# Expert rounds of a two-layer MoE backbone, unrolled and overlapped across rounds (Trainium2, one core)

## What is computed

```python
def expert_choice_ffn(h, router_w, w1, w3, w2):
    bsz, n, d = h.shape
    cap = n * EC_CAPACITY // N_EXPERTS              # 32 tokens for each of 16 experts
    aff = jax.nn.softmax((h @ router_w).astype(F32), axis=-1)
    gates, idx = lax.top_k(jnp.swapaxes(aff, 1, 2), cap)
    ...
    xe = jnp.take_along_axis(h, idx[..., None], axis=1).reshape(bsz, N_EXPERTS, cap, d)
    hid = jax.nn.silu(jnp.einsum('becd,edf->becf', xe, w1)) * jnp.einsum('becd,edf->becf', xe, w3)
    ye = jnp.einsum('becf,efd->becd', hid, w2) * gates[..., None].astype(h.dtype)
    return jnp.zeros_like(h).at[jnp.arange(bsz)[:, None], idx].add(ye.reshape(bsz, N_EXPERTS * cap, d))
```

## Time and profile before

| | us |
|---|---|
| median of 3 runs (2564.57 to 2569.61) | 2565.92 |
| the profiled execution, its own time | 2568.53 |
| its span on the core | 2566.8 |
| TensorE busy (share of the span) | 2026.7 (79%) |
| VectorE busy | 779.4 (30%) |
| ScalarE busy | 514.3 (20%) |
| DMA, mean over the span | 205 GB/s |
| chain that ended last: transfers of expert weights | 23% |
| chain that ended last: expert products (L883) | 11% |

### The profile page before, as it was taken

How to read it: one execution, slowest core, us unless ns; L and a number is a source line. 1 busy time by engine, 2 the same in 40 slices (tenths; PEclk the granted TensorE clock), 3 DMA queues, 4 the chain that set the end, 5 groups by cost and what they waited for, 6 DMA issues and landing times.

```text
span 2566.8 us, 31156 instructions
## 1 busy us (share of the span) xinstructions
PE 2026.7 (79%) x12656; PEld 1071.9 (42%) x12656; DVE 779.4 (30%) x1454; ACT 514.3 (20%) x1049; POOL 191.0 (7%) x230
## 2 busy tenths in 40 slices
PE   5899769987799588888888899949997955656655
PEld 1344554434444432323232566627786831212211
DVE  1011453337730310000010577756765120000001
ACT  1223331112210201010000333244442010000000
POOL 0000000012200000000000400004442000000000
PEclk8899889989999799999999999979998977878887
DMA  9701302160041169898989331110001239999996
GB/s 362 274 9 66 131 0 99 66 240 23 1 164 66 67 262 430 341 432 346 431 340 426 139 131 74 66 66 2 2 2 58 93 162 433 432 431 431 429 433 255
DMA packets 57497, 527.07 MB, mean 205 GB/s; under 512 B 2848, under 2 KB 4128, under 8 KB 43040
## 3 DMA queue, kind: packets, MB, share of 16 engines
q1 hardware_dynamic: 55760, 522.55, 49.1%
q10 hardware_dynamic: 1616, 2.76, 0.3%
HBM read 524.26 MB, written 1.05 MB: 205 GB/s over the span
## 4 chain that ended last, share of the span: by engine, by line
PE 54%; DMA 24%; DVE 9%; issue 4%; ACT 3%; SPq 3%; DVEq 1%; PEldq 0%; POOL 0%; POOLq 0%; PEld 0%; ACTq 0%
DMA ring<-in_moe_w 23%; PE bank L432 21%; PE bank L883 11%; PE bank L812 7%; SPq L283 2%; PE bank L868 2%; DVE ring L1581 2%; PE bank L536 2%; PE bank L619 1%; PE bank L642 1%; DVE x L1943 1%; DMA ring<-in_ab_w 1%; PE bank L405 1%; PE bank L929 1%; PE bank L823 1%
## 5 line engine op out<-in xcount | busy, mean ns | idle before, releaser
L432 PE MATMUL bank<-hT,ring 128*128 128x512 f32 (+1 forms) x1504 | 550.9, 524 | 11.4 <-ACT hT L1006 7.2
L883 PE MATMUL bank<-ring,xgs 128*32 128x512 f32 x3072 | 390.8, 666 | 140.4 <-DMA ring<-in_moe_w 132.0
L432 PEld LDWEIGHTS bank<-hT,ring 128*128 128x128 f32 x1504 | 283.8, 191 | 257.3 <-issue 240.1
L883 PE MATMUL bank<-ring,hT 128*32 128x512 f32 x1536 | 209.0, 701 | 95.3 <-DMA ring<-in_moe_w 95.2
L883 PEld LDWEIGHTS bank<-ring,xgs 128*32 128x32 f32 x3072 | 110.6, 121 | 409.1 <-issue 300.4
L1770 DVE TENSOR_TENSOR hT<-sils,bank 128x512 f32<-128x512 f32 x24 | 15.8, 685 | 601.7 <-PEq L911 601.7
L883 PEld LDWEIGHTS bank<-ring,hT 128*32 128x32 f32 x1536 | 57.3, 126 | 241.5 <-issue 191.7
L1776 DVE SCALAR_TENSOR_TENSOR x<-bank,modT,x 128x256 f32<-128x256 f32 x96 | 42.5, 480 | 320.5 <-PE bank L929 320.5
L1435 DVE SCALAR_TENSOR_TENSOR x<-gluR,cols,x 128x256 f32<-128x256 f32 x240 | 116.0, 483 | 15.9 <-issue 0.4
L1244 ACT ACTIVATE sils<-bank 128x512 f32<-128x512 f32 x24 | 13.5, 596 | 331.4 <-PEq L904 331.3
L385 PE MATMUL bank<-ring,act_c 128*32 128x512 f32 x384 | 56.1, 743 | 26.3 <-DMA ring<-in_mod_w 24.5
(11 more groups left out here) (440 smaller groups left out, 2473.6 us busy)
## 6 DMA issues: line engine op xcount, KB each, us to landing
ring<-in_moe_w SPq DMA_DIRECT2D x96, 4096.0 KB, 21.8
ring<-in_mod_w SPq DMA_DIRECT2D x48, 1024.0 KB, 14.2
ring<-in_cd_w SPq DMA_DIRECT2D x6, 4096.0 KB, 17.9
ring<-in_ab_w SPq DMA_DIRECT2D x5, 4096.0 KB, 21.8
ring<-in_ab_wo SPq DMA_DIRECT2D x2, 4096.0 KB, 18.4
ring<-in_cd_wo SPq DMA_DIRECT2D x2, 4096.0 KB, 12.4
x<-in_xT SPq DMA_DIRECT2D x1, 2048.0 KB, 10.2
ring<-in_ab_w SPq DMA_DIRECT2D x1, 2048.0 KB, 15.7
```

Source lines behind the costliest of these rows:

```text
L432: last = mm(ps[p["no"] % 4][:, p["c0"]:T], w[:, k, :], hT[:, k, p["c0"]:T], start=(k == 0), stop=(k == KD - 1))
L883: last = mm(ps[banks + s][32 * j:32 * j + 32, :], lhs[s][:, 4 * kh + k, 32 * j:32 * j + 32], w[:, j, k, :], start=(kh == 0 and k == 0), st ...
```

## The change

The loops over q on TensorE, ScalarE and VectorE become Python loops, so all four rounds stand in the instruction streams one after the other. The operations are the same ones; their order on each engine changes, and `xg` gets a second buffer:
- the scatter steps of round q - 1 stand after the products of groups 0, 1, 2 and 3 of round q, two steps after each;
- the (up to) four half gathers of round q + 1 stand after the products of groups 6, 7, 8 and 9 of round q, in banks 4 and 7 alone;
- only the first round's gather stands ahead of its products, and only the last round's scatter behind them;
- the drains that counted `moe_h1`, `moe_h3` and `moe_y` go, and ScalarE and VectorE wait for `w_used` of the group in their place.

```diff
-            xgs = sb("xgs", [P, 2, KD, P], F32, st)
+            xgs = sb("xgs", [P, 2, 2, KD, P], F32, st)
+        def used(layer, q, gi):
+            return rg.first[f"moe{layer}"] + 12 * q + gi + 1
+        def gathered(layer, streams, q, b):
+            return 16 * layer + 2 * len(streams) * q + b
 # TensorE
-                with pe.Fori(0, Q) as q:
-                    pe.wait_ge(sg("moe_added"), 8 * q + 8 * q0)
...
+                def gather(q, b):
+                    if q >= Q or b >= 2 * len(streams):
+                        return
+                    s, half = streams[b // 2], b % 2
+                    no = gathered(layer, streams, q, b)
+                    if b >= 2:
+                        pe.wait_ge(sg("moe_xg"), no - 1)
+                    elif q > 0:
+                        pe.wait_ge(sg("moe_added"), 8 * (Q * layer + q - 1))
+                    for k in range(4):
+                        ch = (4 * half + k) * P
+                        for tt in range(2):
+                            last = mm(ps[(4, 7)[half]][:, k * P:(k + 1) * P], htok[:, 2 * s + tt, ch:ch + P], pick[:, s, tt, P * q:P * q + P],
+                                      start=(tt == 0), stop=(tt == 1), skip_group_check=True)
+                    last.then_inc(sg("gathered"), 1)
...
+                def scatter(q, steps):
+                    if q < 0:
+                        return
+                    done = Q * layer + q
+                    for dt in steps:
+                        if dt % 4 == 0:
+                            pe.wait_ge(sg("moe_ycopied"), 2 * done + dt // 4 + 1)
+                        if 8 * done + dt >= 2:
+                            pe.wait_ge(sg("moe_added"), 8 * done + dt - 1)
...
+                for b in range(4):
+                    gather(0, b)
+                for q in range(Q):
+                    n = 2 * (Q * layer + q)
+                    pe.wait_ge(sg("moe_xg"), gathered(layer, streams, q + 1, 0))
+                    if n:
+                        pe.wait_ge(sg("moe_tcopied"), n)
+                    product(q, 0, 0, xg[q % 2], 0)
+                    scatter(q - 1, (0, 1))
+                    product(q, 1, 1, xg[q % 2], 0)
+                    scatter(q - 1, (2, 3))
+                    if n:
+                        pe.wait_ge(sg("moe_ycopied"), n)
+                    product(q, 2, 0, xg[q % 2], 2)
+                    scatter(q - 1, (4, 5))
+                    product(q, 3, 1, xg[q % 2], 2)
+                    scatter(q - 1, (6, 7))
+                    pe.wait_ge(sg("moe_silu"), n + 1)
+                    product(q, 4, 0, xg[q % 2], 0)
+                    product(q, 5, 1, xg[q % 2], 0)
+                    turn(q, 0, 5)
+                    product(q, 6, 0, xg[q % 2], 2)
+                    gather(q + 1, 0)
+                    product(q, 7, 1, xg[q % 2], 2)
+                    gather(q + 1, 1)
+                    pe.wait_ge(sg("moe_tcopied"), n + 1)
+                    product(q, 8, 0, hidT, 5)
+                    gather(q + 1, 2)
+                    turn(q, 1, 0)
+                    product(q, 9, 0, hidT, 2)
+                    gather(q + 1, 3)
+                    pe.wait_ge(sg("moe_tcopied"), n + 2)
+                    product(q, 10, 1, hidT, 5)
+                    product(q, 11, 1, hidT, 2)
+                scatter(Q - 1, range(KD))
 # ScalarE: gate waits for w_used of group 4 * hf + 1, result for that of group 10 + hd
+                for b in range(4):
+                    gather(0, b)
+                for q in range(Q):
+                    gate(q, 0)
+                    gate(q, 1)
+                    turned(q, 0)
+                    gather(q + 1, 0)
+                    gather(q + 1, 1)
+                    gather(q + 1, 2)
+                    turned(q, 1)
+                    gather(q + 1, 3)
+                    result(q, 0)
+                    result(q, 1)
 # VectorE: hidden waits for w_used of group 4 * hf + 3
+                for q in range(Q):
+                    add(q - 1, range(6))
+                    hidden(q, 0)
+                    add(q - 1, (6, 7))
+                    hidden(q, 1)
+                add(Q - 1, range(KD))
```

More of the change, by code:

```diff
@@ L854, in experts @@
                 first = rg.first[f"moe{layer}"]
-                q0 = Q * layer
-                with pe.Fori(0, Q) as q:
-                    pe.wait_ge(sg("moe_added"), 8 * q + 8 * q0)
[L859 to L889, removed]
-                        for s in streams:
[L891 to L923, removed]
@@ new lines, in product @@
+                def product(q, gi, kh, lhs, banks):
+                    s = (first + gi) % RING
+                    pe.wait_ge(landed[s], q * 64 + rg.landed[first + gi])
+                    w = ring[:, s, :, :].rearrange("p j (k n) -> p j k n", k=4)
+                    for k in range(4):
+                        for s in streams:
+                            for j in range(4):
+                                last = mm(ps[banks + s][32 * j:32 * j + 32, :], lhs[s][:, 4 * kh + k, 32 * j:32 * j + 32],
+                                          w[:, j, k, :], start=(kh == 0 and k == 0), stop=(kh == 1 and k == 3),
+                                          tile_position=(0, 32 * j))
+                    last.then_inc(w_used, 1)
@@ new lines, in turn @@
+                def turn(q, hf, bank):
+                    pe.wait_ge(sg("moe_hid"), 2 * (Q * layer + q) + hf + 1)
+                    for s in streams:
+                        for b in range(4):
+                            last = nc.tensor.transpose(ps[bank + s][:, b * P:(b + 1) * P],
+                                                       hid[s][:, 512 * hf + b * P:512 * hf + b * P + P], ident[:, :])
+                    last.then_inc(sg("moe_turned"), 1)
+                def scatter(q, steps):
[3 more added lines that the diff above has]
+                    for dt in steps:
@@ L1230, in experts @@
             def experts(layer, streams):
[L1231 to L1256, removed]
@@ new lines, in gather, with gate @@
+                def gather(q, b):
+                    if q >= Q or b >= 2 * len(streams):
+                        return
+                    s, half = streams[b // 2], b % 2
+                    act.wait_ge(sg("gathered"), gathered(layer, streams, q, b) + 1)
+                    A_(xg[q % 2][s][:, 4 * half:4 * half + 4, :], ps[(4, 7)[half]].rearrange("p (k c) -> p k c", k=4),
+                       ACT.Copy).then_inc(sg("moe_xg"), 1)
+                def gate(q, hf):
+                    n = 2 * (Q * layer + q) + hf
+                    act.wait_ge(w_used, used(layer, q, 4 * hf + 1))
+                    if n:
+                        act.wait_ge(sg("moe_hid"), n)
+                    for s in streams:
+                        last = A_(sil[s], ps[s], ACT.Silu)
+                    last.then_inc(sg("moe_silu"), 1)
```

46 lines of the change are left out of this document (28 added, 18 removed).

## The result

The change takes 2531.14 us (median of 4 runs, 2528.47 to 2532.02) against 2565.31 us (median of 4, 2564.57 to 2569.61): a ratio of 0.9862 with a 95% interval of 0.9845 to 0.9879. That is 34.2 us faster, where 40.9 were forecast, and 6.1 us over the forecast time of 2525.0. The profiled execution took 2530.77 us with a span of 2529.0; the span before was 2566.8, so these two differ by 37.8, and 3.1 of the 40.9 us are missing there. That 37.8 is more than 34.2 comes mainly from the profiled execution of before, which lay 3.2 us over its median. The change measured once more, in a later set of runs, gave 2531.13 us against 2567.52 (0.9863, 0.9839 to 0.9887). In what follows, a ratio stands behind each time, with its 95% interval; it is to the kernel before, measured beside it.

What follows compares the result with a forecast made beforehand. Layer 0 was taken as bound by DMA inside rounds and TensorE's serial tail at three boundaries, layer 1 by its weights. 2568.5 - 40.9 = 2527.6 us for the profiled execution, 2525.0 against the median; range 2517 to 2540.

Steps and rivals of the forecast that it cites:

- The bound and its hole: Layer 0: DMA-bound inside rounds, a load hole of some 10 us at three boundaries costing 13.7 each; layer 1 has none.
- the ring: Layer 0 boundaries: three weight loads run on after a round's last group lands; then loads stop until a slot comes free.
- TensorE's sum: Layer 0: products, gathers, scatter and turns take 104.1 us a round, 109.3 with changes of form, below the DMA's 116.6.
- The 5.2 us for 18 changes of form: Layer 0, per round: switches between 32-column and full matmuls, 18 against 6 before, 0.29 us each at the worse end.
- The new waits: Waits of moved scatter, gather and copies on adds, copies and banks: no releaser later than its place in the product stream; 0.
- The stall at the loop's top: TensorE wait of 4.61 us without a releaser at a layer 0 boundary; goes with the loop, no separate gain.
- the 24.5 us: Serial boundary between layer 0 rounds: scatter of 8.29 us, rest of its adds, a stall of 4.61 us, and the gather.
- The sum: Layer 0: with loads never stopped, group 47 lands 349.7 us after group 11 started, at 1363.7 against 1404.64; gain 40.9 us.
- Layer 1, which I had at 0: Layer 1: transfers saturated from first round to last, so the overlap has no hole to fill; gain 0.
- A: Layer 0 partial gain: TensorE late from tile changes or a missed wait a round; gain 20 to 25 us, 2543; chance 0.09.
- B: No gain: loads stop elsewhere or the code does not overlap as written; rounds stay at 130 us, 2566; chance 0.03.
- C: Slower: unrolled streams are fetched anew, each fetch stalling TensorE 4.61 us in layer 0; +53 us, 2619; chance 0.05.

## Why the prediction was right, and where it was off

**The bound and its hole: right.** Layer 0 lost its time in a hole of the loads at three boundaries, layer 1 lost none. After the change the DMA share is 1.00 through rounds 1 to 3, and three other ways to shorten the boundary (17.4, 8.0 and about 8.3 us) gave what the ring says each should.

**TensorE's sum: right in size, its terms less so.** 104.1 us a round were forecast and 104.0 measured. That they agree to 0.1 us is luck: the gathers took 8.2 us in place of 9.1 (24.6 for three), since they no longer ran at the boundary's lower clock, and two products a round took 8.6 to 8.8 in place of 7.07. The 5.2 us for 18 changes of form were too many. I had taken the worse end, which came from a scatter behind a drain; the starts give 2.9 at most, and these are inside the 104.0. The room was 12.6 us. The Trainium skill says that changing the tiling mode drains TensorE (TensorEngine Tiling (Array Packing), Key Properties). The traces neither show nor exclude a drain: if there is one, it is part of the 0.16 us.

**The new waits: right.** None of them has idle time in the profile but the first gather's last copy, 0.7 us, as before.

**The stall at the loop's top: misjudged in what it was worth.** As "part of the 24.5 us" it could not change the sum, but the loop cost more than 4.61: with the lower clock and the slower gather behind the stall it took 7.1 us of the first boundary. Had the change been only to unroll, my reading would have said 14 us and the chip 25.

**The sum: the step that failed** is "with the loads never stopped, group 47 lands 36 x 9.714 = 349.7 us later". It landed 354.3 us later. 9.714 us was read from layer 1 before, where one page of instructions was fetched in those 36 loads; layer 0 fetches 22 in the same stretch. At 0.2 us each, as measured in layer 1, they would cost 4.4 us (an estimate; no version fetched fewer in layer 0). They were there before the change too, 27 in the same loads, and cost little, because each hole let the slower engines catch up: the distance between a load's first and last engine fell to 0.8 to 1.0 us behind each hole and never passed 2.1 us in layer 0 before, and it is at most 2.2 in the unrolled kernel with the serial order, which keeps a hole. Without holes the delays add up, to 6.4 us. This took 4.6 us of the 40.9. Layer 1, which I had at 0, lost 1.5 us in the same way: its loop fetched 1 packet, and unrolled it fetches 11. What came the other way is 1.5 us from the last product (7.1 in place of 8.60, which the forecast left open and no version was made to test), 0.3 to 0.5 from an earlier start, and 0.8 in the stages between the layers. With a product of 8.60 again, the missing part would have been larger, so the nearness of 37.8 to 40.9 is in part luck. That leads to the 37.8 us between the two profiles:

```text
                                              before     after      earlier by
first product of layer 0 starts               915.07     914.76       0.3
last load of layer 0 lands                   1404.60    1367.80      36.8
norm behind layer 0 starts (L405, L413)      1423.60    1384.97      38.6
first product of layer 1 starts              2095.56    2056.17      39.4
last product of layer 1 starts               2540.49    2503.01      37.5
```

**The rivals.** A and B did not come. C had the right suspect and the wrong victim: pages do cost something when a loop is unrolled, but TensorE has no idle time for one inside the rounds; the weights' loads are held back. The Trainium skill (Runtime: NRT & Kernel Launch, Instruction fetch mechanics) says that sequential code is streamed ahead and that a taken branch stalls where its target has to be fetched. The traces agree on both for TensorE (no idle time without a releaser inside unrolled rounds, 5.5 us at the old loop's top).

What stays open is why just these engines are hit. The traces don't name a packet's engine, only the landings. A version that fetches fewer pages in layer 0 was not tried, since the body of four experts' matmuls is itself the code.

## What to carry to other kernels

With loads that run through a ring, a serial stretch costs only what exceeds the loads under way, so moving the first part of it gives everything and the rest nothing: compute how long the ring lasts before moving more. Here, with three slots and 9.71 us a load, a product could start some 8 us behind its load's landing at no cost. That holds inside a round as well as between rounds: with the scatter three times, work that was 1 us a round over the DMA's total cost 7 us in all, because it was bunched behind four products. When holes in a saturated stream are closed, take the rate from a stretch with as many instruction packets, not from a quieter one; compare the loads in which a packet starts with the others, and look at the distance between the first and the last of a load's 16 landings. Removing a loop is worth more than the stall at its top where TensorE's clock falls in that stall.

## What the runs showed that I had not expected

Instruction packets slow a saturated load stream by about 0.2 us each (1.4 us for 7, 1.6 for 9, 16 KB each; 3.2 to 3.4 us for 14 of 8 KB on the other queue), although the packets are 0.2% of the bytes, and only the loads in which one starts are slow. The landings read as if a single DMA engine carried each. The engines drift apart from 1.9 us to 4.0 (11 packets), 6.4 (22) and 10.4 (41), though not by the same amount in every kernel with as many, and they came back together in each hole of the loads. And of the added waits on a semaphore that is already met, the traces hold half; GpSimd took so long over them that TensorE waited 66 us for a stage behind it.
